# A two-layer streaming encoder on one core: first norm's sums by token, weights loaded between token blocks, two gap columns dropped

## The chip, the cores and the metric

One core of a Trainium2 chip runs the whole program. The metric is device time in microseconds (us) of one launch. The engines are TensorE (PE, matmuls; its weight loads are listed as PEld), VectorE (DVE), ScalarE (ACT), GpSimd (POOL) and SyncE (SP, which here only starts transfers). Transfers are started on three queues: SP's, ACT's and POOL's.

## The reference

1024 prompt tokens and 32 sample tokens of width 1024 go through two layers. Layer 0 mixes tokens by chunked attention with 16 heads and a learned relative-position bias, layer 1 by a gated MLP with position mixing (gMLP); a ConvFFN follows each mixer. All is float32.

```
def rms_norm(x, g):
    y = x * rsqrt(mean(x * x, axis=-1) + EPS)
    return y * g

# layer i (DEPTH = 2); prompt and sample tokens go the same way
h = rms_norm(x, ln_mix[i])
x = x + (band_attn(h) if i % 2 == 0 else gmlp(h))
x = x + conv_ffn(rms_norm(x, ln_ffn[i]))
...
y = rms_norm(x, ln_final)

def conv_ffn(h, hist, w_up, conv_w, conv_b, w_down):
    a = h @ w_up                         # 1024 -> 5632
    full = concat([hist, a])             # 2 rows of history (zeros for the prompt)
    c = conv_b + sum(full[:, j:j + T] * conv_w[j] for j in range(3))
    gate, val = split(c)
    return (silu(gate) * val) @ w_down
```

In attention a chunk of 64 queries sees its own and the 8 chunks before it: softmax(q k / 8 + bias) v, then `@ w_o`. The bias is a table of 257 distances per head.

## The kernel before, in words

**Layout.** Activations are kept transposed, features on the 128 partitions and tokens along the free axis: `x[P, 8, TW]`, with `TW` = 1058 columns: 1024 prompt tokens, 2 gap columns (`GAP`), 32 sample tokens. The gap holds zeros in `x`; in the ConvFFN's buffers it is the place of the sample's two history rows, so that one shifted access does the convolution of both. Columns are worked on in three chunks, `CH`, of 352, 352 and 354.

**Matmuls.** A product in float32 precision is three passes: the operand's high part (`gx_hi`, `w_hi`) and its rest (`gx_lo`, `w_lo`), as hi*hi + hi*lo + lo*hi (`product`, lines 156 to 158). A weight is split by ACT (`w_hi`, a copy with rounding) and DVE (`w_lo`, the difference). `linear` does the 8 feature tiles of a chunk, 24 matmuls. The norm's factor per token (`rstd`) is multiplied in as the product leaves PSUM, so PE need not wait for it; only `gx_hi` and `gx_lo` (x times the gain, lines 215 and 221) must be there.

**The start.** Nine token blocks (eight of 128 tokens, one of 32) arrive in token layout (`xin`), even ones on SP's queue and odd ones on ACT's. PE transposes each in two halves of four tiles (`turn_block`, line 381); ACT copies the first half to `x` (line 426) and DVE the second (line 444). A transpose of block b waits for the copies of block b - 2, which used the same PSUM banks. When a chunk's blocks are there, ACT makes, tile by tile, `gx_hi` and a square (`act_tile`, line 212), DVE `gx_lo`, and POOL adds the squares of the 8 tiles up in `total` (`Norm.pool`, lines 230 and 233). Two `squares` buffers stand between, so a square waits for the add of the one but one before it. A matmul with `ones` then sums over the partitions (`pe_sum`, line 238), and DVE, ACT and DVE again turn the sum into `rstd` over all 352 columns: mean, root, reciprocal.

**The steps.** The first head pair needs nine steps `first_pe(o)`, o from 0 to 8, a chunk of v, k or q each, in the order of `FIRST`: v and k of chunk 0, v and k of chunk 1, v and k of chunk 2, then q of all three. Steps use PSUM banks 6 and 7 in turn, so step o waits for the output of step o - 2 (`first_out`, lines 959 and 981). Steps 0 and 1 stand in `input_pe` behind block 5, the others behind block 8 in `attention_pe`; extra transposes of v, k and the parameters lie between the later ones.

**Other work at the start.** ACT's queue also loads the ConvFFN's taps and history (8 small loads). POOL makes constants, then stores the expanded bias table to DRAM (`bias_scratch`, 16 heads x 64 copies, line 367), waits for that, reads it back shifted into `bias` (line 371), and only then adds squares. SP issues the weights of v, k and q (`load_unit`, line 598) behind its token blocks; a slot of `raw0` is loaded again when its weight has been split.

**Behind it.** Eight head pairs of attention with the projections of the next pair laid between (a loop over pairs), ConvFFN 0 (22 feature pairs over two layers, 11 loop turns each: 12 groups of 24 matmuls up, 24 groups of 6 down), gMLP, ConvFFN 1, the last norm. The later norms sum by columns already (`pe_columns`, `dve_columns`, `pe_spread`): a matmul gives each token's sum on its own partition, the roots are taken there, and `ones` times a diagonal matrix of the factors (DVE, line 276) spreads them over the partitions again.

The order on each engine is written out by hand; semaphores tie them. Memory regions are shared over time: the attention's tiles lie where `xin` was, so what overwrites `xin` waits until it is read.

## Time and profile before

| | us |
|---|---|
| median of 3 runs | 2728.03 (2728.01 to 2732.96) |
| span of the profiled execution | 2726.1 |
| around the span, to the median (the profiled execution's own time is not listed) | 1.9 |
| PE busy | 2609.6 (96%) |
| DVE busy | 1610.8 (59%) |
| ACT busy | 902.6 (33%) |
| POOL busy | 256.6 (9%) |
| mean granted PE clock | 0.983 |

The span is from the first to the last instruction. Busy times of engines overlap. Matmuls are pipelined: an instruction's listed time is longer than the distance to the next, so the pace is read from starts. A granted clock of 1 is 2.4 GHz, 0.5 is 1.2 GHz.

### The profile page before, as it was taken

The numbers are of one execution on the slowest core, as the hardware profiler recorded it, in microseconds if no ns is written. First come the engines' busy times: TensorE is split into PE (matmuls) and PEld (weight loads), VectorE is DVE, ScalarE is ACT, GpSimd is POOL, SyncE is SP. The second block draws the span as 40 slices with busy tenths as digits, with TensorE's granted clock in tenths as the row PEclk, the third lists the DMA queues.
The fourth block names the chain that finished last, engine by engine and source line by source line (L and its number), as shares of the span: only waits on it lengthen the run. The fifth ranks groups of instructions, "written<-read, shape, count | busy, mean of one in ns | idle before, by whom it ended". The sixth has DMA issues, their size and how long they took to land.

```text
span 2726.1 us, 43489 instructions
## 1 busy us (share of the span) xinstructions
PE 2609.6 (96%) x15757; PEld 2524.9 (93%) x15757; DVE 1610.8 (59%) x3213; ACT 902.6 (33%) x1711; POOL 256.6 (9%) x583
## 2 busy tenths in 40 slices
PE   4999999999789999999999999999999999999998
PEld 4888888888669999999999999999899999999998
DVE  5565566656566666666666552332666666666666
ACT  4333433343353222222222353132522222222223
POOL 4000000000030000000000042122100000000003
PEclk8999999999889999999999999999999999999999
DMA  4111111110001111111111121111111111111111
GB/s 130 44 36 37 32 32 41 36 36 21 24 16 47 47 46 46 46 46 46 46 46 46 31 64 31 32 33 46 63 47 46 45 37 41 46 46 46 46 44 76
DMA packets 99451, 120.66 MB, mean 44 GB/s; under 512 B 3676, under 2 KB 87844, under 8 KB 99332
## 3 DMA queue, kind: packets, MB, share of 16 engines
q1 hardware_dynamic: 94972, 108.06, 12.3%
q0 software_dynamic: 3088, 8.67, 1.1%
q10 hardware_dynamic: 1272, 2.39, 0.3%
q8 instruction: 69, 1.13, 0.2%
q14 instruction: 50, 0.41, 0.0%
HBM read 108.70 MB, written 10.40 MB: 44 GB/s over the span
## 4 chain that ended last, share of the span: by engine, by line
PE 88%; DVE 4%; ACT 3%; POOL 2%; issue 2%; DMA 1%; DVEq 0%; ACTq 0%; POOLq 0%
PE psum L156 25%; PE psum L158 25%; PE psum L157 25%; PE psum L770 4%; PE psum L809 2%; PE psum L754 2%; POOL total L233 2%; PE psum L806 1%; PE psum L1588 1%; DVE x L1050 1%; DMA bias_scratch<-rel_rev 1%; DVE gx_lo L221 1%; PE psum L692 0%; ACT conv_t L1277 0%; ACT v L703 0%
## 5 line engine op out<-in xcount | busy, mean ns | idle before, releaser
L156 PE MATMUL psum<-gx_hi,w_hi 128*128 128x352 f32 (+1 forms) x3264 | 1075.6, 330 | 13.8 <-DVE stage L959 4.1
L158 PE MATMUL psum<-gx_hi,w_lo 128*128 128x352 f32 (+1 forms) x3264 | 1062.6, 326 | 0.0
L157 PE MATMUL psum<-gx_lo,w_hi 128*128 128x352 f32 (+1 forms) x3264 | 1062.5, 326 | 0.0
L156 PEld LDWEIGHTS psum<-gx_hi,w_hi 128*128 128x128 f32 x3264 | 618.9, 190 | 19.8 <-issue 8.0
L157 PEld LDWEIGHTS psum<-gx_lo,w_hi 128*128 128x128 f32 x3264 | 618.1, 189 | 2.3 <-issue 0.7
L158 PEld LDWEIGHTS psum<-gx_hi,w_lo 128*128 128x128 f32 x3264 | 619.4, 190 | 0.0
L1364 DVE TENSOR_TENSOR x<-x,psum 128x352 f32<-128x352 f32 (+1 forms) x528 | 259.7, 519 | 120.9 <-PE psum L158 120.9
L1277 ACT ACTIVATE conv_t<-a_gate,cur 128x352 f32<-128x352 f32 x132 | 90.1, 683 | 539.6 <-DVE a_gate L1334 539.3
L156 PE MATMUL psum<-h_hiA,w_hi 128*128 128x352 f32 (+1 forms) x528 | 171.8, 325 | 4.1 <-DVE x L1364 4.1
L156 PE MATMUL psum<-h_hiB,w_hi 128*128 128x352 f32 (+1 forms) x528 | 172.0, 326 | 0.0
L158 PE MATMUL psum<-h_hiA,w_lo 128*128 128x352 f32 (+1 forms) x528 | 171.1, 324 | 0.0
L157 PE MATMUL psum<-h_loA,w_hi 128*128 128x352 f32 (+1 forms) x528 | 170.8, 323 | 0.0
L157 PE MATMUL psum<-h_loB,w_hi 128*128 128x352 f32 (+1 forms) x528 | 170.6, 323 | 0.0
L158 PE MATMUL psum<-h_hiB,w_lo 128*128 128x352 f32 (+1 forms) x528 | 170.5, 323 | 0.0
L1169 DVE TENSOR_TENSOR w_lo<-raw,w_hi 128x1024 fp32r<-128x1024 f32 x132 | 160.9, 1219 | 12.3 <-ACT w_hi L1166 12.3
L1334 DVE TENSOR_TENSOR a_gate<-psum,rstd 128x352 f32<-128x352 f32 (+2 forms) x176 | 72.1, 431 | 146.2 <-PE psum L158 143.3
L1166 ACT ACTIVATE w_hi<-raw 128x1024 fp32r<-128x1024 f32 x132 | 136.0, 1045 | 2.0 <-PE psum L158 1.9
L1341 DVE SCALAR_TENSOR_TENSOR conv_t<-a_gate,cur,conv_t 128x352 f32<-128x352 f32 x132 | 77.4, 586 | 99.2 <-ACT conv_t L1277 99.0
L897 ACT ACTIVATE pT<-psum 128x512 f32<-128x512 f32 (+2 forms) x160 | 78.9, 505 | 155.4 <-PE psum L754 154.4
L770 PE MATMUL psum<-pT,v 128*128 128x256 f32 (+1 forms) x496 | 126.9, 386 | 0.0
L1277 ACT ACTIVATE conv_t<-a_val,cur 128x352 f32<-128x352 f32 x132 | 90.2, 683 | 105.0 <-DVE a_val L1334 105.0
L1282 ACT ACTIVATE s_gate<-conv_t 128x352 f32<-128x352 f32 x132 | 65.9, 499 | 165.9 <-DVE conv_t L1344 165.9
(180 smaller groups left out, 3447.2 us busy)
## 6 DMA issues: line engine op xcount, KB each, us to landing
raw<-in_f_w_up SPq DMA_DIRECT2D x44, 1024.0 KB, 5.1
raw<-in_f_w_down SPq DMA_DIRECT2D x22, 1024.0 KB, 4.9
raw<-in_a_w_qkv SPq DMA_DIRECT2D x24, 512.0 KB, 3.8
raw<-in_b_w_in SPq DMA_DIRECT2D x8, 1024.0 KB, 5.4
raw<-in_a_w_o SPq DMA_DIRECT2D x8, 512.0 KB, 3.5
raw<-in_b_w_out SPq DMA_DIRECT2D x4, 1024.0 KB, 5.0
out<-raw SPq DMA_DIRECT2D x6, 512.0 KB, 2.7
xin<-in_x_prompt SPq DMA_DIRECT2D x4, 512.0 KB, 5.4
```

The source lines that it names most:

```text
L156: pe.matmul(out, w[0], rhs[0], start=first, stop=False)
L157: pe.matmul(out, w[0], rhs[1], start=False, stop=False)
L158: return pe.matmul(out, w[1], rhs[0], start=False, stop=last)
L770: mm = pe.matmul(psum[:, bank, :width], v, pT[:rows, slot, 2 * P * i:2 * P * i + width], start=(kb == blocks[0]), stop=(kb == blocks[-1]))
L897: act.activation(dst, src, ACT.Copy).then_inc(t_free, 1)
L1166: act.activation(shape(f_hi[slot]), self.raw_of(u), ACT.Copy).then_inc(self.w_hi, 1)
L1169: dve.tensor_tensor(shape(f_lo[slot]), self.raw_of(u), shape(f_hi[slot]), ALU.subtract)\
L1277: act.activation(conv_t[:, o % 2, :n], a_buf[g][:, start + 2:start + 2 + n], ACT.Identity, scale=cur[:, 2, g, i:i + 1], bias=cur[:, 3, g, ...
L1282: act.activation(s_gate[:, start:start + n], conv_t[:, o % 2, :n], ACT.Silu).then_inc(self.silu, 1)
L1334: mm = dve.tensor_tensor(a_buf[g][:, a + 2:b + 2], psum[:, o % RING, a - start:b - start], rstd[:, a:b], ALU.mult)
L1341: dve.scalar_tensor_tensor(t, a_buf[g][:, start + 1:start + 1 + n], cur[:, 1, g, i:i + 1], t, ALU.mult, ALU.add).then_inc(self.conv1, 1)
L1364: mm = dve.tensor_tensor(chunk(x[:, d, :], c), chunk(x[:, d, :], c), psum[:, n % RING, :CH[c][1]], ALU.add)
```

## The change

The first norm is summed in token layout: as a block arrives, ACT squares it whole with an accumulator (`first_square`), which gives the token's sum on its partition in `rs_col`; its output goes to unused space in `bias`. For three groups of blocks (0 to 2, 3 to 5, 6 to 8) DVE takes the mean, ACT the root, DVE the reciprocal and the diagonal blocks, PE spreads them by a matmul with `ones`, ACT copies the result to `rstd`. POOL adds nothing here any more. ACT copies the first halves of blocks 0 to 2 alone; DVE copies both halves from block 3 on.

The v and k weights are loaded on SP's queue between token blocks; the taps and history go from ACT's queue to SP's. The bias store waits for token blocks 6 and 7, and SP reads it back, after the last square. Steps 0 and 1 stand behind block 4, and steps 2 to 4 between the later blocks.

`GAP` is no longer in `TW`: 1056 columns, three chunks of 352. The ConvFFN's buffers keep the gap (`AW`), so its convolution of the third chunk still has 354 columns, and the product of gate and value is written in two pieces there. Memory clears of the gap in `rstd`, `x`, `o_hi`, `o_lo` fall away.

```diff
-    TW = SEQ + GAP + DEC
-    SMP = SEQ + GAP
+    TW = SEQ + DEC
+    SMP = SEQ
+    AW = TW + 2 * GAP
     CH = [(0, 352), (352, 352), (704, TW - 704)]
+    CONV_N = [352, 352, TW + GAP - 704]
...
+    ACT_HALVES = 3
+    def turned_by_dve(b):
+        return b + 1 if b < ACT_HALVES else ACT_HALVES + 2 * (b - ACT_HALVES + 1)
...
+    FIRST_CUT = [(0, 3 * P), (3 * P, 6 * P), (6 * P, TW)]
+    def first_square(act, b):
+        n = BLOCKS[b][1]
+        act.wait_ge(x_in[b], 16)
+        at_least(act, first_sq, b)
+        junk = bias[:n, :, :].rearrange("p t v -> p (t v)")[:, :D]
+        act.activation(junk, xin[:n, b, :], ACT.Square, accum_out=rs_col[:n, b:b + 1]).then_inc(first_sq, 1)
+    def first_means(dve, g):
+        dve.wait_ge(first_sq, min(3 * g + 3, NB + 1))
+        for rows, cut in FIRST_COLS[g]:
+            dve.tensor_scalar(rs_col[rows, cut], rs_col[rows, cut], 1.0 / D, EPS, ALU.mult, ALU.add)\
+                .then_inc(first_mean, 1)
+    def first_inverse(dve, g):
...
+            dve.reciprocal(rs_col[rows, cut], rs_col[rows, cut]).then_inc(first_inv, 1)
+        dve.wait_ge(first_inv, FIRST_AT[g + 1])
+        for b in range(3 * g, min(3 * g + 3, NB + 1)):
+            start, n = BLOCKS[b]
+            op = dve.tensor_scalar(total[:n, start:start + n], ident[:n, :n], rs_col[:n, b:b + 1], None, ALU.mult)
+        op.then_inc(first_diag, 1)
+    def first_spreads(pe, g):
+        a, b = FIRST_CUT[g]
+        pe.wait_ge(first_diag, g + 1)
...
+        mm = pe.matmul(psum[:, 4, :last - a], ones[:, :], total[:, a:last], start=True, stop=True)
...
+    def first_rstd(act, g):
+        a, b = FIRST_CUT[g]
+        act.wait_ge(first_spread, g + 1)
+        act.activation(rstd[:, a:b], psum[:, 4, :b - a], ACT.Copy).then_inc(first_ready, 1)
 
     def input_sp(sp):
...
+        block(0)
+        block(2)
+        load_unit(sp, 0, 1, qkv_unit(2, 0))
+        block(4)
+        load_unit(sp, 1, 2, qkv_unit(1, 0))
+        block(6)
         sp.dma_start(xin[:DEC, NB, :], x_sample[0]).then_inc(x_in[NB], 16)
+        for i in range(DEPTH):                      # taps and history: 8 loads, from ACT's queue
...
+        load_unit(sp, 0, 3, qkv_unit(0, 0))
+        sp.wait_ge(rel_out, 16)
+        sp.wait_ge(first_sq, NB + 1)
+        for h in range(2):
...
+            sp.dma_start(bias[CK * h:CK * (h + 1), :, :], src).then_inc(bias_in, 16)
...
         pool.wait_ge(rel_done, 2)
+        pool.wait_ge(x_in[NB - 2], 16)
+        pool.wait_ge(x_in[NB - 1], 16)
         pool.dma_start(bias_scratch, rel_rev[:, None, :].to_broadcast([HEADS, CK, REV])).then_inc(rel_out, 16)
-        pool.wait_ge(rel_out, 16)
...
     def input_pe(pe):
         turn_params(pe, 0)
-        for b in range(NB + 1):
+        for b in range(5):
             turn_block(pe, b)
-            if b == LAST_BLOCK[1]:
-                first_pe(pe, 0)
-                norm_a.pe_sum(pe, 0)
-                first_pe(pe, 1)
+        first_pe(pe, 0)
+        first_pe(pe, 1)
+        first_spreads(pe, 0)
+        for b in (5, 6):
+            turn_block(pe, b)
+        first_pe(pe, 2)
+        first_spreads(pe, 1)
+        first_pe(pe, 3)
+        for b in (7, 8):
+            turn_block(pe, b)
+        first_pe(pe, 4)
+        first_spreads(pe, 2)
 
     def input_act(act):
...
+        for b in range(3):
+            block(b)                                # square, and the first half's copy for b < 3
+        split_act(act, 0)
+        halves(0)                                   # gx_hi of the chunk's 8 tiles
+        split_act(act, 1)
+        first_roots(act, 0)
+        block(3)
+        first_rstd(act, 0)
+        block(4)
+        block(5)
+        halves(1)
+        first_roots(act, 1)
+        block(6)
+        first_rstd(act, 1)
+        block(7)
+        block(8)
+        halves(2)
+        first_roots(act, 2)
+        first_rstd(act, 2)
 
     def input_dve(dve):
...
+        for b in range(3):
+            block(b)
+        split_dve(dve, 0)
+        halves(0)                                   # gx_lo
+        first_means(dve, 0)
+        split_dve(dve, 1)
+        block(3)
+        first_inverse(dve, 0)
+        block(4)
+        first_out(dve, 0)
+        block(5)
+        first_out(dve, 1)
+        first_means(dve, 1)
+        halves(1)
+        first_inverse(dve, 1)
+        block(6)
+        block(7)
+        first_out(dve, 2)
+        block(8)
+        first_means(dve, 2)
+        halves(2)
+        first_inverse(dve, 2)
...
     def attention_pe(pe):
-        for o in range(2, STEPS):
+        for o in range(5, STEPS):
             first_pe(pe, o)
-            if o in (3, 4):
-                norm_a.pe_sum(pe, o - 2)
-            if o in (4, 5):
-                turn_params(pe, o - 3)
-            if o == 5:
+            if o in (5, 6):
+                turn_params(pe, o - 4)
+            if o == 6:
...
-                        pr = prod[:, k_par(c, i), :n]
-                        dve.tensor_tensor(pr, t, s_gate[:, start:start + n], ALU.mult).then_inc(self.prod, 1)
+                        for a, b, at in self.pieces(c):   # two pieces in the third chunk
+                            cut = slice(at - GAP, at - GAP + b - a)
+                            mm = dve.tensor_tensor(prod[:, k_par(c, i), a - start:b - start],
+                                                   conv_t[:, o % 2, cut.start - start:cut.stop - start],
+                                                   s_gate[:, cut], ALU.mult)
+                        mm.then_inc(self.prod, 1)
```

## Rows read from the trace of the kernel before

**Rows 1.** Stretches: window, length, busy us (instructions) per engine, PE clock, DMA share, GB/s.
```profile
0.00:37.30 37.30, 10.70 (x49) 9.64 (x50) 11.56 (x16) 14.32 (x26) 12.68 (x22) 0.77 0.85 223
37.30:73.90 36.60, 29.00 (x154) 27.63 (x153) 23.98 (x28) 18.14 (x38) 18.02 (x18) 0.86 0.05 16
...
840.00:1550.00 710.00, 708.70 (x4385) 708.06 (x4385) 458.43 (x839) 205.82 (x311) 25.52 (x143) 1.00 0.14 46
```

**Rows 2.** Waits, 0 to 95 us: who <- released by: us, times, longest.
```profile
PE psum L381 <- ACT x L426: 17.1, 1, 17.1
...
POOL bias L371 <- DMA bias_scratch<-rel_rev: 15.7, 1, 15.7
...
ACT squares L212 <- POOL total L230: 8.1, 1, 8.1
```

**Rows 3.** Timeline (start, length): first matmuls of steps 0, 5 and of attention.
```profile
37.32 0.64 PE L156 MATMUL psum<-gx_hi,w_hi 128*128 128x352 f32 x1
...
73.97 0.41 PE L156 MATMUL psum<-gx_hi,w_hi 128*128 128x354 f32 x1
...
93.79 0.71 PE L806 MATMUL psum<-kT,qd 128*128 128x64 f32 x4 [1.02 <-DVE qd L981]
```

**Rows 4.** Transfers, 11 to 14 us: packets, MB per queue; issues: KB each, us to landing.
```profile
DMA packets 411, 1.13 MB, mean 378 GB/s; under 512 B 19, under 2 KB 175, under 8 KB 411
...
q10 hardware_dynamic: 165, 0.61, 56.6%
...
q1 hardware_dynamic: 161, 0.09, 10.6%
...
raw<-in_a_w_qkv SPq DMA_DIRECT2D x2, 512.0 KB, 23.8
...
bias<-bias_scratch POOLq DMA_DIRECT2D x2, 384.0 KB, 7.9
```

**Rows 5.** Lines, 0 to 95 us: count | busy us, mean ns | idle before.
```profile
L381 PE MATMUL psum<-ident,xin 128*128 128x128 f32 x64 | 12.8, 378 | 19.7 <-ACT x L426 17.1 <-DMA xin<-in_x_prompt 1.6 <-DVE x L444 1.0
...
L215 ACT ACTIVATE gx_hi<-x,gains 128x352 fp32r<-128x352 f32 x16 | 9.2, 576 | 3.3 <-DVE x L444 3.3
...
L444 DVE COPY x<-psum 128x512 f32<-128x512 f32 x8 | 5.3, 686 | 6.7 <-PE psum L381 6.7
...
L563 ACT ACTIVATE w_hi<-raw 128x1024 fp32r<-128x1024 f32 x4 | 4.1, 1043 | 0.0
...
L238 PE MATMUL psum<-total,ones 128*128 128x352 f32 x4 | 1.5, 458 | 0.0
```

**Rows 6.** Timeline of DVE: one gx_lo, and the nine diagonal blocks of a later norm.
```profile
16.63 0.59 DVE L221 SCALAR_TENSOR_TENSOR gx_lo<-x,gains,gx_hi 128x352 fp32r<-128x352 f32 x1 [0.28 <-ACT gx_hi L215]
...
817.40 1.80 DVE L276 TENSOR_SCALAR total<-ident,rs_col 128x128 f32<-128x128 f32 x9
```

**Rows 7.** Lines, 100 to 180 us: an accumulator's reading on ACT.
```profile
L922 ACT ACTIVATION_READ_ACCUMULATOR p_even<-psum,neg_max 128x1 f32 x8 | 1.5, 192 | 0.0
```

**Rows 8.** Timeline of PE, ConvFFN: starts of groups of 48, 24, 96 and 48 matmuls.
```profile
902.16 0.32 PE L156 MATMUL psum<-gx_hi,w_hi 128*128 128x352 f32 x1
...
909.90 0.32 PE L156 MATMUL psum<-gx_hi,w_hi 128*128 128x354 f32 x1
...
913.79 0.32 PE L156 MATMUL psum<-gx_hi,w_hi 128*128 128x352 f32 x1
...
925.43 0.33 PE L156 MATMUL psum<-h_hiA,w_hi 128*128 128x352 f32 x1
...
940.84 0.33 PE L156 MATMUL psum<-h_hiA,w_hi 128*128 128x354 f32 x1
...
948.68 0.32 PE L156 MATMUL psum<-gx_hi,w_hi 128*128 128x352 f32 x1
```

**Rows 9.** Timeline: gx_lo beside POOL's adds; POOL clearing qd.
```profile
59.22 3.54 DVE L221 SCALAR_TENSOR_TENSOR gx_lo<-x,gains,gx_hi 128x354 fp32r<-128x354 f32 x3
...
63.37 3.75 POOL L631 MEMSET qd<- 128x2176 f32 x2
```

More of the change, by code:

```diff
@@ L90, in build @@
     psum = ctx.enter_context(nc.psum_tensor("psum", [P, 8, BANK], F32))
-    squares = hold("squares", [P, 2, 354])
+    squares = hold("squares", [P, 2, 352])
     total = hold("total", [P, TW])
@@ L226, in pool @@
                 k = KT * c + d
-                pool.wait_ge(self.squared, self.tiles + k + 1)
+                pool.wait_ge(self.squared, self.sums + k + 1)
                 sq = squares[:, k % 2, :CH[c][1]]
@@ L231, in pool @@
                 else:
-                    pool.wait_ge(self.added, self.tiles + k)
+                    pool.wait_ge(self.added, self.sums + k)
                     pool.tensor_tensor(chunk(total, c), chunk(total, c), sq, ALU.add).then_inc(self.added, 1)
-        def pe_sum(self, pe, c):
-            pe.wait_ge(self.added, self.tiles + KT * (c + 1))
-            at_least(pe, self.mean, self.chunks + c)
-            pe.matmul(psum[:, self.bank, :CH[c][1]], ones[:, :], chunk(total, c), start=True, stop=True)\
-                .then_inc(self.summed, 1)
-        def dve_mean(self, dve, c):
-            dve.wait_ge(self.summed, self.chunks + c + 1)
-            dve.tensor_scalar(chunk(rstd, c), psum[:, self.bank, :CH[c][1]], 1.0 / D, EPS, ALU.mult, ALU.add)\
-                .then_inc(self.mean, 1)
-        def act_root(self, act, c):
-            act.wait_ge(self.mean, self.chunks + c + 1)
-            act.activation(chunk(rstd, c), chunk(rstd, c), ACT.Sqrt).then_inc(self.root, 1)
-        def dve_rstd(self, dve, c):
-            dve.wait_ge(self.root, self.chunks + c + 1)
-            dve.reciprocal(chunk(rstd, c), chunk(rstd, c)).then_inc(self.ready, 1)
         COLS = ((slice(0, P), slice(0, NB)), (slice(0, DEC), slice(NB, NB + 1)))
@@ new lines, in first_roots @@
+    def first_roots(act, g):
+        for k, (rows, cut) in enumerate(FIRST_COLS[g]):
+            act.wait_ge(first_mean, FIRST_AT[g] + k + 1)
+            act.activation(rs_col[rows, cut], rs_col[rows, cut], ACT.Sqrt).then_inc(first_root, 1)
+    def first_inverse(dve, g):
+        for k, (rows, cut) in enumerate(FIRST_COLS[g]):
+            dve.wait_ge(first_root, FIRST_AT[g] + k + 1)
+            dve.reciprocal(rs_col[rows, cut], rs_col[rows, cut]).then_inc(first_inv, 1)
[4 more added lines that the diff above has]
+        op.then_inc(first_diag, 1)
@@ new lines, in first_spreads @@
+    def first_spreads(pe, g):
+        a, b = FIRST_CUT[g]
+        pe.wait_ge(first_diag, g + 1)
+        at_least(pe, first_ready, g)
+        last = min(b, SEQ)
+        mm = pe.matmul(psum[:, 4, :last - a], ones[:, :], total[:, a:last], start=True, stop=True)
+        if b > SEQ:
+            mm = pe.matmul(psum[:, 4, SEQ - a:b - a], ones[:DEC, :], total[:DEC, SEQ:b], start=True, stop=True)
+        mm.then_inc(first_spread, 1)
+    def first_rstd(act, g):
+        a, b = FIRST_CUT[g]
+        act.wait_ge(first_spread, g + 1)
+        act.activation(rstd[:, a:b], psum[:, 4, :b - a], ACT.Copy).then_inc(first_ready, 1)
@@ L377, in turn_block @@
         for half in range(2):
-            at_least(pe, (x_act, x_dve)[half], b - 1)
+            if half == 0:
+                at_least(pe, x_act, min(b - 1, ACT_HALVES))
+            if b >= 2 and (half == 1 or b - 2 >= ACT_HALVES):
+                pe.wait_ge(x_dve, turned_by_dve(b - 2))
             for j in range(4):
@@ L438, in input_dve, with block, halves @@
-    def input_dve(dve):
+        first_pe(pe, 0)
[10 more added lines that the diff above has]
+        first_spreads(pe, 2)
+    def input_act(act):
+        def block(b):
+            first_square(act, b)
+            if b < ACT_HALVES:
+                act.wait_ge(x_turned, 2 * b + 1)
+                act.activation(*turned(b, 0), ACT.Copy).then_inc(x_act, 1)
+        def halves(c):
+            for d in range(KT):
+                norm_a.x_ready(act, c, d)
+                norm_a.act_hi(act, c, d)
+        copy_params(act, 0)
+        for b in range(3):
[17 more added lines that the diff above has]
+        first_rstd(act, 2)
@@ L439, in input_dve, with block, halves @@
+    def input_dve(dve):
+        def block(b):
+            for half in range(0 if b >= ACT_HALVES else 1, 2):
+                dve.wait_ge(x_turned, 2 * b + half + 1)
+                dve.tensor_copy(*turned(b, half)).then_inc(x_dve, 1)
+        def halves(c):
+            for d in range(KT):
+                norm_a.dve_tile(dve, c, d)
         dve.wait_ge(rel_in, 16)
@@ L984, in attention_dve @@
     def attention_dve(dve, norm):
-        norm_a.dve_row(dve, 1)
-        for o in range(2, STEPS):
-            if o == 4:
-                norm_a.dve_row(dve, 2)
+        for o in range(3, STEPS):
             if o == 6:
@@ L1616, in v_set @@
                 if first and o < 2:
-                    act.wait_ge(Norm.added, norm.tiles + NCH * KT)
+                    act.wait_ge(Norm.added, norm.sums + NCH * KT)
                 else:
@@ L1846, in y_sums @@
     def y_sums(pe, group):
-        pe.wait_ge(Norm.added, norm_e.tiles + KT * (NCH - 1 + group))
+        pe.wait_ge(Norm.added, norm_e.sums + KT * (NCH - 1 + group))
         for b in Y_GROUPS[group][0]:
@@ L1998, in _ @@
         input_pool(pool)
-        for c in range(NCH):
-            norm_a.pool(pool, c)
         attention_pool(pool)
```

155 lines of the change are left out of this document (57 added, 98 removed).

## The prediction

> **What bounds the kernel now.** I read the page first: TensorE (PE) is busy in 2609.6 of 2726.1 us, so the end can only move where PE stands idle or where its matmuls get shorter. The view by stretches says where it is idle [rows 1]: in 840 to 1550 us, the first ConvFFN, PE works 708.7 of 710.0 us and every other engine has slack (DVE 458.4); in the first 37.3 us it works 10.7, and in the next 36.6 us 29.0, at a granted clock of 0.86. So the change has two places: the start, up to the first attention matmul at 93.79 us [rows 3], and the width of the third chunk everywhere behind it.
>
> The view of waits over the start names the chain [rows 2]. PE's longest idle time, 17.1 us, ends when ScalarE (ACT) copies a transposed block. ACT was late because a square of the first norm waited 8.1 us for GpSimd (POOL) to add the one before, and POOL began to add only after 15.7 us of waiting for the bias table's store into DRAM, which stands ahead of the adds in its program. Then ACT still had squares and weight splits to do before PE's first projection step began at 37.32 us. The fifth further on, called step 5 (the steps count from 0), began at 73.97, and attention 19.8 us after that [rows 3].
>
> **The change part by part.** I rebuild the time of step 5 in the new order, because from there on PE's work is the old one.
>
> Loads. By the packet counts of 11 to 14 us each queue gets one packet in turn: 165 of ACT's and 161 of SP's, though 0.61 MB against 0.09, as a weight's packets are an eighth of a token block's [rows 4]. SP's queue now holds blocks 0 and 2, the v weight, block 4, the k weight, block 6. The v weight's 1024 small packets therefore outlast the 512 large ones of blocks 1, 3, 5, 7 on ACT's queue. So it lands when 3.67 MB are through: at 378 GB/s [rows 4] 9.7 us, from a start of the loads near 2.5 us, 12.2; I take 14.0, as ACT's queue starts later, behind the gains, and small packets end the transfer. Bounds: 8.5 if the queues shared by bytes, and 27.2, where it lands now (issue at 3.4 plus 23.8, [rows 4]) with the bias store beside it; the store now waits for blocks 6 and 7. The estimate is nearest to the first, since what slowed that row is gone. The k weight comes after another 1.05 MB, about 17.5, before ACT wants it.
>
> Step 0. Before 14.0 ACT has done three squares of whole token blocks and three copies, until 13.1; that it issues eight loads less ahead of them gains nothing, since it then waits for the weight. A square of 1024 columns is not in the trace; a split of that width takes 1.04 [rows 5] and reading an accumulator 0.19 [rows 7], so 1.25, not below 1.04 and not above 1.6 (a half again). PE has turned five blocks by 17.3 (12.8 us for eight blocks, [rows 5]). From 14.0: split of v 1.04, eight gx_hi of 0.576 [rows 5] to 19.7, split of k to 20.7. DVE follows with w_lo of v and eight gx_lo of 0.59 [rows 6], is through at 21.1, and makes w_lo of k (no longer than the gap of 1.2 to 22.4). Step 0 ends at 21.7 in their shadow. The square's adds on POOL, 24 of them, are gone, and with them the wait of 8.1.
>
> Steps 1 to 4. Step 1 from 22.4: 24 matmuls are 7.74 / 2 = 3.87 us [rows 8], with its drain 4.0, to 26.4. The spread of the first 384 columns takes 0.85 (the old sums of 352 columns took 0.75, 1.5 us for two, [rows 5]), the copy to rstd on ACT no more than a gx_hi, 27.9. Here is the new wait: ACT stands 3.4 us at that copy, and squares 4 and 5 (2.5 us) and eight gx_hi (4.6) queue behind it, to 35.0; the last gx_lo is done at 35.7, the three diagonal blocks cost DVE 0.6 (a third of 1.80, [rows 6]) and a reciprocal 0.16, 36.4. PE, which turned blocks 5 and 6 meanwhile and did step 2 at DVE's pace, spreads until 37.3 and does step 3 until 41.4. Then it turns blocks 7 and 8, 1.1 us to the second half; DVE copies both halves (0.69 each, [rows 5]) to 43.3, puts out step 2 (0.5, no more than a gx_lo) and copies the small block 8, 44.4; one gx_hi and eight gx_lo of the third chunk end at 49.7, the reciprocals and diagonals at 50.6, the spread at 51.5, where step 5 starts. I add 0.5 for PE's clock: PE will stand idle 2.1 us at 29.5 and 2.7 us at 43, and the stretch with such gaps now has 0.86 [rows 1]. So 52.0 instead of 73.97.
>
> To attention. From step 5 the old order took 19.8 us; a transpose of parameters (0.4) moves behind step 5 and a few copies stand differently, so 20.4: attention at 72.4 instead of 93.79. Saved: 21.4.
>
> What this costs elsewhere is nothing, under these covers. The bias band is read back by SP after the last square (40.4) and after the store, which starts at 20 and is waited for 15.7 us now [rows 2], so is through by 36; the two reads land about 7.9 us after issue [rows 4], near 49, and are wanted at 73. Behind those waits on SP stands one weight of the next head pair, wanted at 60. The parameters' loads, now on SP behind the tokens, are wanted at 56. Clearing qd on POOL (3.75 us, [rows 9]) lies at 44 to 48 beside DVE's gx_lo of the third chunk. Beside POOL's two-input adds gx_lo takes 1.18 [rows 9] instead of 0.59; the long clears of the trace lie beside one-input work only. A clear reads nothing, so I take 0, and keep 3.75 / 1.18 x 0.59 = 1.9 as the other end. The Trainium skill, GPSIMD Engine Reference, section Specifications, says that GpSimd shares its SBUF interfaces with VectorE and contends with instructions of two SBUF inputs, and exempts no kind of GpSimd work; gx_lo is such an instruction, so by that rule the 1.9 would be paid.
>
> Two columns less. A third-chunk group of 24 matmuls takes 913.79 - 909.90 = 3.89 us, one of 352 columns 3.87: 23 ns less in finer digits. In the down projection 48 matmuls of the third chunk take 7.84, of the others (940.84 - 925.43) / 2 = 7.71 [rows 8], of which I count only the same 23 ns a group, as the rest may belong to the loop's turn. Groups: ConvFFN 22 x (4 + 2) = 132, attention 8 x 4 = 32, gMLP 24: 188 x 23 ns = 4.3 us. Bounds: 0 (not the columns) and 22 x (130 - 46) ns more, 6.2. The Trainium skill, TensorE: Matmul & The Clock Gate, section Wait — 56ns, not 53.3ns?, gives N / 2.4 GHz + 2.5 ns from start to start: 149 ns for 352 columns, where the trace has 161 [rows 8], so its level does not hold here; its slope would make the saving 3.8.
>
> The extra half product per value tile on DVE (44 times) is hidden by the 251 us that DVE is free in 710 [rows 1]; uncovered, at a whole 0.59 each, it would be 26 us.
>
> The sum: -21.4 - 4.3 = -25.7. The profiled span of 2726.1 has some 1.9 us around it to the median of the runs, 2728.0; 2728.0 - 25.7 = 2702.3.
>
> **The rivals.** (a) The weights come late: each us of the v weight beyond 14.0 moves step 5 by one, as the chain starts there. For it: small packets lose by turns [rows 4]; against it: nothing is left beside them. At 18 to 24: 2706 to 2712. (b) PE's clock stays at the lower of its two levels until 26 us, through steps 0 and 1: step 1 then takes 7.0 instead of 3.9, and 0 is late too, 5.4 together: 2707.7. For it: [rows 1] has 0.77 for the first stretch; against it: PE now works from 7 us almost without a gap. (c) DVE pays beside the clears: 2704.2. (d) Slower: the bias band becomes the wait. DVE's first attention step needs both reads; if SP's smaller pieces and the store behind the tokens bring them past 73 + 25.7 = 99 us, the kernel loses one us per us: at 105, 2734. Against it: 58 us between issue and that point, where two reads take 7.9 now. (e) The start isn't shortened because another wait takes the gap, say the spread's copy in ACT's order holding blocks 7 and 8 back: only the columns stay, 2723.7 or no change.
>
> **How the numbers follow.** The forecast has 0.72, with an own range of 2698 to 2706; (a) 0.11, (b) 0.08, (c) 0.04, (d) 0.03, (e) 0.02. The range 2697 to 2711 reaches from both gains at their best (6.2 for the columns, the v weight by 13, where ACT is free, no clock loss: 2698.9, and some 2 us of what the parts leave open) into most of (a) and all of (b) and (c). 0.2% is 5.5 us, about what a measurement here can tell from no change. Faster by more than that: 0.95; within: 0.02; slower: 0.03.
>
> **What would show it.** Step 5's first matmul near 52 and attention near 72; POOL without adds before 80 us; the v weight's split starting at 14; ACT waiting some 3 us once, for the first spread; a third-chunk group at the length of the others. Wrong: the split of v after 18, step 1 at 7 us, gx_lo of 1.18 between 45 and 50, or DVE waiting for the bias.

## The result, and the profile after

The changed kernel takes 2695.94 us (median of 4 runs, 2693.13 to 2698.9) against 2729.01 for the kernel before beside it (2728.01 to 2732.96): a ratio of 0.9874, 95% interval 0.986 to 0.9888. That is 33 us less; the profiled spans, 2726.1 and 2691.4, differ by 34.7. The forecast was 25.7 less, and the time lies 1.1 us below the low end of the range. The direction was right, and the start saved about what was forecast, in part by luck; one term of the sum, the columns, was given a third of what it measured.

Stretches of the kernel after, to be held against [rows 1] (window, length, busy us and instructions of PE, PEld, DVE, ACT, POOL, PE clock, DMA share, GB/s):

```profile
0.00:37.30 37.30, 25.70 (x147) 23.48 (x148) 20.27 (x42) 24.25 (x45) 2.45 (x10) 1.00 0.83 202
37.30:73.90 36.60, 32.14 (x193) 30.75 (x192) 17.13 (x43) 12.94 (x28) 8.14 (x11) 0.91 0.35 88
840.00:1550.00 710.00, 705.71 (x4380) 705.12 (x4379) 458.55 (x857) 216.00 (x337) 40.25 (x155) 1.00 0.13 43
...
40.00:50.00 10.00, 7.45 (x34) 7.37 (x34) 7.12 (x21) 4.13 (x10) 3.77 (x2) 0.66 0.64 131
```

PE works 25.7 of the first 37.3 us instead of 10.7. The last row is the stretch in which its clock was at the lower of its two levels (0.66 on the mean): it fell at 42.3 us, while PE stood 2.55 us for the third chunk (40.7 to 43.2), and rose at 49.2.

PE's timeline after, against [rows 3] (start, length): first matmuls of steps 0 and 5 and of attention.

```profile
16.80 0.40 PE L157 MATMUL psum<-gx_hi,w_hi 128*128 128x352 f32 x1 [0.40 <-DVE gx_lo L216]
...
50.70 0.43 PE L157 MATMUL psum<-gx_hi,w_hi 128*128 128x352 f32 x1
...
70.77 0.32 PE L881 MATMUL psum<-kT,qd 128*128 128x64 f32 x1 [1.09 <-DVE qd L1055]
```

Attention starts 23.0 us earlier (93.79 - 70.77). The other 11.7 come behind it. PE's starts in the first ConvFFN, against [rows 8], matmul for matmul:

```profile
872.22 0.32 PE L157 MATMUL psum<-gx_hi,w_hi 128*128 128x352 f32 x1
...
879.90 0.32 PE L157 MATMUL psum<-gx_hi,w_hi 128*128 128x352 f32 x1
...
883.74 0.32 PE L157 MATMUL psum<-gx_hi,w_hi 128*128 128x352 f32 x1
...
895.26 0.32 PE L157 MATMUL psum<-h_hiA,w_hi 128*128 128x352 f32 x1
...
910.86 0.32 PE L157 MATMUL psum<-h_hiA,w_hi 128*128 128x352 f32 x1
...
918.63 0.32 PE L157 MATMUL psum<-gx_hi,w_hi 128*128 128x352 f32 x1
```

Read the distances: the third chunk's group took 3.89 and takes 3.84. But the 48 matmuls of the first two chunks, whose width is the same in both kernels, took 7.74 and take 7.68, and the 96 of the down projection with unchanged width went the other way, 15.41 to 15.60. So the pace changed of matmuls that the change leaves as they are. A whole turn of this loop took 69.79 us and takes 69.45; there are 22 turns, 7.6 us.

Over the whole trace PE's matmul time at full clock (busy time less half of what fell into stretches at the lower level) is 12.8 us less: some 7 of it in the two ConvFFNs, 3 in the gMLP between them, 2 in attention and the rest at the end. With the 23.0 of the start that is 35.8; idle time behind the start is 2.1 longer and the clock there costs 0.9 less, which leaves 34.6. These two can't be put to the change: in the last head pair alone, where PE idles some 24 us in every kernel of this study, the lower clock cost 13.6 us before, 9.1 after, and between 8 and 15 in the others. The start varies with the clock too: in the seven kernels below that keep the changed kernel's order and move only addresses or columns, attention began between 67.9 and 72.3 us.

### The profile page after: what moved, and what is told of

It reads as the page before. It is cut to its first block, busy times and chain, and to the rows that moved or that the text cites. A ratio compares the mean times of both kernels' runs of the same rounds, so it can differ in the third digit from the quotient of the medians.

```text
span 2691.4 us, 43514 instructions
## 1 busy us (share of the span) xinstructions
PE 2592.8 (96%) x15759; PEld 2509.1 (93%) x15759; DVE 1604.1 (60%) x3274; ACT 898.7 (33%) x1703; POOL 240.0 (9%) x553
## 4 chain that ended last, share of the span: by engine, by line
PE 88%; DVE 4%; ACT 3%; POOL 2%; issue 2%; DMA 0%; ACTq 0%; DVEq 0%; POOLq 0%
PE psum L157 25%; PE psum L159 25%; PE psum L158 25%; PE psum L845 4%; PE psum L884 2%; POOL total L228 2%; PE psum L829 2%; PE psum L881 1%; PE psum L1666 1%; DVE x L1121 1%; DVE gx_lo L216 1%; PE psum L770 0%; ACT conv_t L1350 0%; ACT v L781 0%; DVE gx_lo L1825 0%
## 5 line engine op out<-in xcount | busy, mean ns | idle before, releaser
L157 PE MATMUL psum<-gx_hi,w_hi 128*128 128x352 f32 x3264 | 1073.3, 329 | 17.1 <-DVE gx_lo L216 7.0
L158 PE MATMUL psum<-gx_lo,w_hi 128*128 128x352 f32 x3264 | 1058.4, 324 | 0.0
L159 PE MATMUL psum<-gx_hi,w_lo 128*128 128x352 f32 x3264 | 1057.8, 324 | 0.0
L1442 DVE TENSOR_TENSOR x<-x,psum 128x352 f32<-128x352 f32 x528 | 258.9, 516 | 122.4 <-PE psum L159 122.4
L157 PE MATMUL psum<-h_hiA,w_hi 128*128 128x352 f32 x528 | 172.3, 326 | 4.3 <-DVE x L1442 4.3
L157 PE MATMUL psum<-h_hiB,w_hi 128*128 128x352 f32 x528 | 172.5, 327 | 0.0
L159 PE MATMUL psum<-h_hiB,w_lo 128*128 128x352 f32 x528 | 171.9, 326 | 0.0
L159 PE MATMUL psum<-h_hiA,w_lo 128*128 128x352 f32 x528 | 171.4, 325 | 0.0
L158 PE MATMUL psum<-h_loA,w_hi 128*128 128x352 f32 x528 | 170.6, 323 | 0.0
L158 PE MATMUL psum<-h_loB,w_hi 128*128 128x352 f32 x528 | 170.4, 323 | 0.0
```

What stands on the lines that cost most here:

```text
L157: pe.matmul(out, w[0], rhs[0], start=first, stop=False)
L158: pe.matmul(out, w[0], rhs[1], start=False, stop=False)
L159: return pe.matmul(out, w[1], rhs[0], start=False, stop=last)
L1442: mm = dve.tensor_tensor(chunk(x[:, d, :], c), chunk(x[:, d, :], c), psum[:, n % RING, :CH[c][1]], ALU.add)
```

## The experiments

**Where the pace comes from.** The tiles lie one behind the other in a partition, so a narrower row moves all that follows: by the tiles' sizes, rows of `gx_hi` and `gx_lo` stand 4224 bytes apart in the changed kernel (33 x 128) and 4232 before, and its weights (`raw0`, `w_hi`, `w_lo`) begin 32 bytes beyond a multiple of 64, where they began on one before. "Turn" is the distance of one matmul in two turns of the ConvFFN loop, "up" (1024 to 5632 features) and "down" (back to 1024) the mean distance of matmuls in ns, worked out from starts over a turn's 288 and 144; they come out alike in every turn, to 0.05 us. "Weights" says where the tiles begin: x64 at a multiple of 64 bytes, +32 beyond one by 32. "Single" marks one run; a time also holds what the clock cost in that execution, so the reading goes by the turn. (Some expectations quote 160.3 up and 161.6 down for the kernel after; those means had taken in matmuls of the neighbouring group. The table has it right: 160.0 and 162.3.)

| kernel | columns | rows apart | weights | turn us | up | down | time us |
|---|---|---|---|---|---|---|---|
| before | 1058 | 4232 | x64 | 69.79 | 161.6 | 161.5 | 2729.0 |
| before_pitch1064 | 1058 | 4256 | x64 | 69.74 | 161.4 | 161.5 | 2726.0 |
| before_pitch1072 | 1058 | 4288 | x64 | 69.80 | 161.6 | 161.5 | 2728.1 |
| before_cols | 1056 | 4224 | +32 | 69.45 | 160.0 | 162.3 | 2718.8 |
| after | 1056 | 4224 | +32 | 69.45 | 160.0 | 162.3 | 2695.9 |
| after_n354 | 1056, up 354 | 4224 | +32 | 69.71 | 160.9 | 162.2 | 2705.4 single |
| after_pitch1058 | 1056 | 4232 | +32 | 70.02 | 161.9 | 162.4 | 2715.2 |
| after_pitch1064 | 1056 | 4256 | +32 | 69.89 | 161.5 | 162.4 | 2711.3 |
| after_w01 | 1056 | 4224 | up x64, down +32 | 69.18 | 159.0 | 162.4 | 2679.9 single |
| after_w64 | 1056 | 4224 | x64 | 68.73 | 159.2 | 159.0 | 2682.7 |
| w64_pitch1058 | 1056 | 4232 | x64 | 69.32 | 161.2 | 159.0 | 2694.4 single |
| w64_pitch1072 | 1056 | 4288 | x64 | 69.27 | 160.9 | 159.3 | 2691.9 single |

before_cols: the column hunks of the diff alone, on the kernel before.

> The kernel before with the two gap columns dropped and nothing else: the start, its sums, loads and order are the old ones. From here on the pace is read from one turn of the ConvFFN loop, the distance of the same matmul in two turns, 69.79 us before and 69.45 after. Theory (the third term of the sum, the columns, was mis-sized and is worth 12.7 us at full clock, not 4.3): the turn falls to 69.45 and the time to 2716, 12 to 14 us less, while attention still starts near 93.8. Rival (the columns are worth the 4.3 that the prediction gave them, and the rest of the gain comes from the start or from chance in the clock): the turn falls to 69.65, the time to 2724 to 2725.

Turn 69.45; 2718.8 us, ratio 0.9966 (0.9952 to 0.998). PE's work at full clock fell by 13.0, as after; attention began 2.0 us later (95.78 against 93.79). The time fell by 11.2 against the kernel before beside it (2730.0), a little under the 12 to 14 expected. The first theory holds: the columns' hunk is worth some 13 of PE's work, and the start the rest. The first matmuls of two turns:

```profile
942.96 0.32 PE L158 MATMUL psum<-gx_hi,w_hi 128*128 128x352 f32 x1
...
1012.41 0.32 PE L158 MATMUL psum<-gx_hi,w_hi 128*128 128x352 f32 x1
```

after_pitch1058, after_pitch1064, before_pitch1064, before_pitch1072: only the distance of rows.

```
-    gx_hi = hold("gx_hi", [P, KT, TW], F32R)
+    gx_hi = hold("gx_hi", [P, KT, 1058], F32R)[:, :, :TW]     # gx_lo alike; 1064, 1072 in the others
```

> The changed kernel with its 1056 columns, but the rows of gx_hi and gx_lo stand 1058 columns apart as before (4232 bytes instead of 4224; 4224 is a multiple of 64, 4232 is not). Same instructions, same columns, only the addresses of the moving operand differ. Theory (the row distance sets the pace of all groups, the narrow ones too: 161.25 ns from matmul to matmul before against 159.98 after at the same 352 columns): the groups go back to 161.2 or so, the turn of the ConvFFN to 69.7, the time rises by 6 to 9 us, to 2702 to 2705. Rival (fewer columns and lighter traffic of the other engines make the pace): turn 69.45, time 2696, as after.

> The changed kernel with rows of gx_hi and gx_lo 1064 columns apart (4256 bytes, a multiple of 32 and not of 64). Theory of the row distance, first form (every row must begin at a multiple of 64 bytes): half the rows are off, so the turn lies between 69.5 and 69.7 and the time 3 to 6 us over the changed kernel's. Second form (multiples of 32 do): turn 69.45, time 2696. Rival (the row distance is nothing): 69.45 and 2696 as well, but then the run with 1058 shows it too.

> The kernel before with its 1058 columns and its old start, and only the rows of gx_hi and gx_lo 1064 columns apart instead of 1058 (4256 bytes instead of 4232). Theory of the row distance, if multiples of 32 bytes do: the groups of 352 columns go from 161.25 to 160.0 ns a matmul, the turn falls from 69.79 to 69.5, the time by 6 to 9 us to 2720 to 2723, with not one column less. If multiples of 64 are wanted: about half of that. Rival (columns alone): turn 69.79, time 2728 to 2729.

> The kernel before with all its 1058 columns and its old start; only the rows of gx_hi and gx_lo stand 1072 columns apart (4288 bytes, a multiple of 64; to make room rel_rev lies where kout is written later). Theory (rows must begin at multiples of 64 bytes; the columns themselves are worth next to nothing): the groups of 352 columns go from 161.4 to 160.0 ns a matmul, those of 354 to 160.9, the turn of the ConvFFN falls from 69.79 to 69.46 us, and the time to 2717 to 2719, like that of the kernel with the columns dropped, with not one column less. Rival (it takes the 1056 columns, or another address that moved with them): turn 69.74 to 69.79, time 2726 to 2730.

In the changed kernel the distance matters, and more than expected: with rows 4232 apart it is at 2715.2 (0.9951 of before, 0.9934 to 0.9969), with 4256 at 2711.3, where 2702 to 2705 and 2699 to 2702 were expected; and its turn of 70.02 with 4232 is worse than before's though it has fewer columns. Some other address had to be at fault too. In the kernel before the distance gives little (2726.0 with 4256) or nothing (4288): that expectation of mine failed, and the form "a multiple of 64 is enough" with it. Here are the first matmuls of two turns of after_pitch1058:

```profile
949.49 0.32 PE L157 MATMUL psum<-gx_hi,w_hi 128*128 128x352 f32 x1
...
1019.51 0.32 PE L157 MATMUL psum<-gx_hi,w_hi 128*128 128x352 f32 x1
```

after_w64 and after_w01: the weights.

```
+    hold("gap0", [P, 8])                          # 32 bytes, in both
     raw0 = hold("raw0", [P, 2048])
```

after_w64 has 32 bytes more ahead of `h_hiA`, after_w01 96 behind the second `w_lo` instead.

> The changed kernel with 32 unused bytes ahead of raw0, so that the weights' tiles raw0, raw1, w_hi and w_lo begin at multiples of 64 bytes as before (in the changed kernel they begin 32 beyond one); 32 more ahead of h_hiA keep the h tiles where they were, at multiples of 64. Theory (weights off the 64 bytes cost as rows of gx do: the run with 1058 columns between rows had a longer turn than before, 70.02 against 69.79, though its columns are fewer, and the weights' addresses are what was left): the second feature pair's group and the down projection, which still vary (161.25 and 161.64 ns), come to 160.0 to 161, the turn falls from 69.45 to 69.1 to 69.3, the time by 3 to 8 us to 2688 to 2693. Rival (only rows of the moving operand count, weights are loaded whole beside the matmuls): turn 69.45, time 2696.

> The changed kernel with 32 unused bytes ahead of raw0 and 96 behind the second w_lo, so that only raw0, w_hi and w_lo 0 and 1 move onto multiples of 64 bytes; these are the weights of the 12 groups up. Everything else (squares, total, the ConvFFN's and the h tiles, and the weights of the down projection) keeps its place modulo 64. Theory (the address of the weights that a matmul loads sets its pace): the groups up go from 160.3 to 159.0 ns a matmul as in the run with all weights moved, the down projection stays at 161.6; turn 69.06 to 69.1. Rival (the other engines' tiles, which moved too in that run, disturbed PE's reads less): groups up stay at 160.3, turn 69.45.

after_w64 runs in 2682.7 us, 0.983 of before (0.9813 to 0.9846), 13 us under the changed kernel, for 32 bytes that nobody reads; that is more than the theory gave (turn 68.73 against 69.1 to 69.3, time 2688 to 2693). Its timeline over one turn, up from 916.34 and down from 962.18:

```profile
916.34 0.32 PE L158 MATMUL psum<-gx_hi,w_hi 128*128 128x352 f32 x1
...
962.18 0.33 PE L158 MATMUL psum<-h_hiA,w_hi 128*128 128x352 f32 x1
...
985.08 0.32 PE L158 MATMUL psum<-gx_hi,w_hi 128*128 128x352 f32 x1
```

after_w01 splits it within one run: the groups up, whose weights moved, go from 160.0 to 159.0; the down projection, whose weights and tiles kept their place, stays at 162.4. Its timeline (groups up from 936.94 and 983.22, down from 959.83):

```profile
936.94 0.32 PE L159 MATMUL psum<-gx_hi,w_hi 128*128 128x352 f32 x1
...
959.83 0.33 PE L159 MATMUL psum<-h_hiA,w_hi 128*128 128x352 f32 x1
...
983.22 0.32 PE L159 MATMUL psum<-gx_hi,w_hi 128*128 128x352 f32 x1
...
1006.12 0.32 PE L159 MATMUL psum<-gx_hi,w_hi 128*128 128x352 f32 x1
```

983.22 to 1006.12 is 22.90 us for 144 matmuls, 159.0 each; 959.83 to 983.22 is 23.39 for as many, 162.4. So the address of the weights acts on the pace by itself. The single time of after_w01 is no measure of it: its turns are 0.27 us shorter than after's, 6 us over 22, and the other 10 of its 16 us go mostly with the clock: the lower level cost it nothing at the start, where it cost the kernel after 3.0, and 22.3 behind it instead of 29.0.

w64_pitch1058 and w64_pitch1072: both at once.

> The kernel with all weights at multiples of 64 bytes, and only the rows of gx_hi and gx_lo 1058 columns (4232 bytes) apart instead of 1056. Theory (the place of the moving rows sets the pace as the weights' place does, each on its own): the groups up go from 159.1 back to 161 or so, as before (161.6 and 160.9 for its groups of 352), the down projection stays at 159.1; turn 69.3 to 69.4. Rival (once the weights stand well the rows don't matter): 159.1 both, turn 68.73.

> The kernel with all weights at multiples of 64 bytes, and rows of gx_hi and gx_lo 1072 columns (4288 bytes, a multiple of 64 and not of 128) apart. The kernel before with this distance gained nothing (161.0 and 160.4 ns in its groups of 352, 163.3 in those of 354). Theory 64 (multiples of 64 do; what held that run up was its 354 columns and other tiles): groups up stay at 159.1, turn 68.73. Theory 128 (rows must begin at multiples of 128 or at least all alike): groups up at 160.4 to 161, turn 69.1 to 69.3.

With good weights the rows still count: 4232 gives 161.2 up, 4288 gives 160.9, and 4224 gives 159.2, while the down projection, whose rows were left alone, stays at 159.0 to 159.3. One turn of w64_pitch1058:

```profile
920.60 0.32 PE L158 MATMUL psum<-gx_hi,w_hi 128*128 128x352 f32 x1
...
967.03 0.32 PE L158 MATMUL psum<-h_hiA,w_hi 128*128 128x352 f32 x1
...
989.92 0.32 PE L158 MATMUL psum<-gx_hi,w_hi 128*128 128x352 f32 x1
```

Theory 128 holds so far as that goes: of the three distances run with such weights (4256 was not) only the multiple of 128 gave the best pace. The down projection's rows all begin 64 beyond a multiple of 128 in after_w64 and do as well, so rows that are all alike may be what counts; that was not tried.

after_n354: the two columns by themselves, at the same addresses.

```
+            rhs = (wide(flat_hi, k), wide(flat_lo, k)) if more else ...   # 354 columns, up, third chunk
```

> The changed kernel, every tile at its place modulo 128, but the ConvFFN's groups up of the third chunk stream 354 columns again (the two more are the next row's first, and nobody reads what comes of them). So it measures the two columns by themselves, 88 groups of 24 matmuls. As in the prediction (23 ns a group, 0.96 ns a matmul): the group goes from 3841 to 3864 ns, the turn of the ConvFFN from 69.45 to 69.54 us. If the columns bring more than their share of time (one more line of the tile to read, as 163.3 against 160.7 ns in the groups of 354 and 352 of the kernel before with rows 1072 apart): 3900 to 3920 ns a group, turn 69.7. In either case the groups of 352 columns stay at 160.0.

```profile
950.50 0.32 PE L159 MATMUL psum<-gx_hi,w_hi 128*128 128x352 f32 x1
...
958.18 0.32 PE L159 MATMUL psum<-gx_hi,w_hi 128*128 128x354 f32 x1
...
962.08 0.32 PE L159 MATMUL psum<-gx_hi,w_hi 128*128 128x352 f32 x1
```

The group of 354 takes 3.90 us against 3.84 in the kernel after, in finer digits 3902 against 3841: 61 ns, not 23. The groups of 352 beside it stay at 160.0 to 160.2. That is the second theory's size; its reason, one more line to read, is not shown.

**What made the start.** after_bias_early and after_weights_late undo one part each, before_adds_first does one on the kernel before.

```
 after_bias_early:   -        pool.wait_ge(x_in[NB - 2], 16); pool.wait_ge(x_in[NB - 1], 16)
 after_weights_late: blocks 0, 2, 4, 6, sample, then load_unit of v and k
 before_adds_first:  pool.wait_ge(rel_out, 16) and the two reads behind norm_a.pool(pool, c)
```

> The changed kernel with one edit undone: the bias table's store into DRAM doesn't wait for token blocks 6 and 7 and is issued near 7 us again, beside the token blocks and weights. Theory (its bytes are in the way: before, block 7 landed at 23.4 and the v weight at 25.7, and now by 18.2 and 13.8): the v weight lands 3 to 6 us later, step 0 begins at 20 to 23 instead of 16.8, attention at 74 to 77 instead of 70.8, time 2699 to 2702. Rival (the store hurt only because POOL's adds waited behind it, and the adds are gone): step 0 at 16.8 to 17.5, time 2696.

2701.6 us, step 5 at 57.04, attention at 77.07: with the bytes of the store in the way the start is 6.3 us longer, part of it by the clock (three stretches of 3.4 us at the lower level against one of 6.8). But the bytes did not act where I had put it. The v weight landed at 12.9, as after (12.35); block 4 landed at 19.3 instead of 14.3, so step 0 began at 20.4, and ACT then waited for the k weight:

```profile
ACT w_hi L647 <- DMA raw<-in_a_w_qkv: 6.5, 1, 6.5
```

> The changed kernel with one edit undone: the v and k weights are issued on SP's queue behind all its token blocks and the sample, as before, not between them. Theory (the chain starts with the v weight, as the prediction's rival (a) said: one us later is one us later): the weight lands near 17.5 instead of before 13.9, step 0 begins at 20 to 21, step 5 at 53 to 55 instead of 50.7, time 2698 to 2701. Rival (ACT has squares left to do meanwhile, and PE's wait for the third chunk takes it up): step 0 late by 3 to 4, but step 5 at 51 and the time 2696 to 2697.

2699.5 us, step 0 at 19.33, step 5 at 53.91. The v weight landed at 16.35; ACT was free for it at 13.85, so 2.5 of its 4 us counted, and step 0 moved by as much. Step 5 moved by 3.2 and the time by 3.6; the further 0.7 lies within what the clock does to a start (at the lower level for three stretches of 3.4 us here, for one of 6.8 in the kernel after). So rival (a) of the prediction is real, about one for one, counted from the moment ACT is free.

> The kernel before with one edit at the start: POOL issues the bias table's store as before, but waits for it and reads it back behind the first norm's adds, not ahead of them. Nothing else moves. Theory (the long idle time of PE at the start was that wait, reached through the squares): the 8.1 us of ACT for POOL's first add go, step 0 begins at 29 to 30 instead of 37.3 and attention near 86, time 2720 to 2723; the rest of the 23 us is then the weights' and the sums' part. Rival (the weights, which landed at 25.7 and 29.4 behind the store, are the next wait, and POOL's adds beside DVE and the bias band that comes later take the rest back): step 0 at 33 to 36, time 2726 to 2730.

2723.7 us, ratio 0.9976 (0.9967 to 0.9986): step 0 begins at 31.14 and attention at 88.63, 5.2 us earlier. That lies between the theory (29 to 30, near 86) and the rival (33 to 36): the long wait on POOL, by itself, was about a quarter of the start's gain. What is late next is PE's wait for a transposed block, and behind it the v weight, which landed at 25.5:

```profile
PE psum L383 <- ACT x L428: 12.6, 1, 12.6
```

**Two better versions.** after_order_w64 has the weights' 32 bytes and another order at the start; `final` adds one wait on POOL.

```
 input_pe:   step 1; turn 5; spread 0; turn 6, 7, 8; step 2; spread 1; steps 3, 4; spread 2
 input_act:  squares 3 to 5, roots 1, squares 6, 7, rstd 0, gx_hi of chunk 1, copies 6, 7, square 8, ...
+        pool.wait_ge(first_diag, 3)               # final: ahead of the clears of qd
```

> The best version I can form from the runs: all weights at multiples of 64 bytes, and a new order at the start. PE turns block 5 ahead of the first spread and blocks 6, 7, 8 ahead of step 2 (block 8 into a bank of its own), then does steps 2, 3 and 4 in a row; ACT squares blocks 3 to 7 while it would wait for the first spread and copies the first halves of blocks 6 and 7; DVE makes the second group's diagonals before the third group's copies. Theory (in the changed kernel PE stands 2.3 us for gx_lo of the second chunk and 2.6 for the third, and pays 3.0 more as its clock falls to half from 42.3 to 49.2): step 2 at 29 to 30, step 5 at 42 to 44 instead of 50.0, attention at 62 to 64 instead of 70.1, time 6 to 8 us under the 2682.7 of the run with the weights moved alone, so 2674 to 2677. Rival (ACT, with two more copies and a square ahead of the third chunk, or DVE is late instead): step 5 at 47 to 50, time 2679 to 2683.

2672.7 us, 0.9792 of before (0.9778 to 0.9805), a little better than expected: step 5 at 43.95, attention at 63.95. The clock stayed at its upper level through this start; against after_w01, where it did too and attention began at 67.86, the new order is worth 3.9. One thing went against plan: DVE's last three diagonal blocks took 3.5 us instead of 0.6 to 0.7. DVE's and POOL's timelines (start, length):

```profile
25.28 0.68 DVE L351 TENSOR_SCALAR total<-ident,rs_col 128x128 f32<-128x128 f32 x3
...
34.44 3.77 POOL L719 MEMSET qd<- 128x2176 f32 x2 [15.91 <-DVE x L523]
...
35.00 3.50 DVE L351 TENSOR_SCALAR total<-ident,rs_col 128x128 f32<-128x128 f32 x3
...
39.13 0.40 PE L158 MATMUL psum<-gx_hi,w_hi 128*128 128x352 f32 x1 [1.56 <-DVE gx_lo L217]
```

> The version with the weights at multiples of 64 bytes and the new order of the start, and POOL's clear of qd held until DVE has made the third group's diagonals. In that version the three diagonal blocks took DVE 3.5 us instead of 0.6 while POOL cleared qd from 34.4 to 38.2, and PE then stood 1.56 us for gx_lo of the third chunk; eight gx_lo beside the same clear in the changed kernel took 0.58 each as ever. Theory (a one-input DVE instruction of that kind and the clear exclude each other, a two-input one and the clear don't): the diagonals take 0.6 to 0.7, gx_lo stay at 0.57 beside the clear, step 4 begins at 37.4 to 37.6 instead of 39.13, step 5 at 42.3 to 42.5 instead of 43.95, time 1.5 us less. Rival (the clear is paid by gx_lo instead): gx_lo at 1.2, step 5 at 44, no gain.

```profile
35.17 0.62 DVE L351 TENSOR_SCALAR total<-ident,rs_col 128x128 f32<-128x128 f32 x3
...
35.72 4.04 DVE L217 SCALAR_TENSOR_TENSOR gx_lo<-x,gains,gx_hi 128x352 fp32r<-128x352 f32 x8
...
35.90 3.77 POOL L720 MEMSET qd<- 128x2176 f32 x2 [17.04 <-DVE total L351]
...
42.26 0.43 PE L158 MATMUL psum<-gx_hi,w_hi 128*128 128x352 f32 x1
```

The diagonals take 0.62 again, the gx_lo beside the clear 4.04 for eight as without it, and step 5 begins at 42.26. The time is 2670.6 us, 0.9781 of before (0.9768 to 0.9795); the step of 1.7 shows in the trace, in the times (2672.7 to 2670.6) it is within their spread. This version is some 25 us faster than the changed kernel.

## Why the prediction missed

**The term that failed** is "Two columns less". It took the difference of a group of 354 and a group of 352 in the old trace, 23 ns, as the price of two columns, times 188 groups: 4.3, at most 6.2. PE's work fell by 12.8. after_n354 gives the price at equal addresses, for the ConvFFN's groups up: 61 ns. (188 x 61 ns would be 11.5, but the down projection, attention and gMLP were not tried.) The old trace hid it because its groups of 352 were themselves slow (7.74 us for 48, 161.25 ns each, where after has 160.0 and after_w64 159.2): their rows stood 4232 bytes apart. w64_pitch1058 shows that this is enough: with weights at multiples of 64, as before, and that distance alone put back, the groups up are at 161.2 again. The reference of the subtraction was spoilt, and the bounds, 0 to 6.2, came from the same rows. The prediction also treated the groups of unchanged width as unchanged; of the 347 ns of a turn they gained 70 (249 up, less 178 lost down, where the weights now stood 32 beyond), and the third chunk's six groups the other 277 instead of 138. Outside the ConvFFN the prediction had 0.6 for the gMLP and 0.7 for attention, where the traces have some 3 and 2; which of their groups gained was not looked into.

The Trainium skill, TensorE: Matmul & The Clock Gate, section Wait — 56ns, not 53.3ns?, has a pace of N / 2.4 GHz + 2.5 ns; its slope would make two columns 20 ns a group, where after_n354 has 61, and its level for 352 columns is 149 ns, where the best of the kernels here has 159.0. The measurements decide against both.

**The start** was forecast to save 21.4 and saved 23.0. Two errors of the sum offset each other, overlap and clock, so the agreement is in part luck. By its steps:

- The v weight's split began at 13.85, forecast 14.0, but not for the forecast reason. The weight landed at 12.35 and waited for ACT, whose squares and copies took until then (forecast 13.1); the prediction had the weight end that wait. Its load sum, 12.2, also came out by luck: it let the weight outlast all four blocks of ACT's queue, and blocks 5 and 7 landed after it, at 13.49 and 15.06. Packet counts as of one packet of each queue in turn stand from 9 to 12.35 us (278 of SP's, 283 of ACT's), but not from 6 to 9, where SP's queue (q1) moved far more packets than ACT's (q10; packets, MB, share):

```profile
q1 hardware_dynamic: 755, 0.65, 69.7%
q10 hardware_dynamic: 115, 0.46, 41.3%
```

- Step 1 began at 21.47 (22.4) and the spread's copy at 26.24 (27.3 to 27.9), with ACT waiting 3.8 for it (3.4): the new wait was there, at its place. It was not the only one: ACT waited 1.4 and 4.8 for the other two spreads, and the 4.8, behind the third chunk, cost PE nothing before step 5. Step 3 at 34.89 (37.3). The sum ran long mainly because an eight of gx_hi was counted as 8 x 0.576: 0.576 is one instruction's length, but they overlap, and eight take 3.95.

```profile
14.98 3.95 ACT L210 ACTIVATE gx_hi<-x,gains 128x352 fp32r<-128x352 f32 x8
...
16.07 4.05 DVE L216 SCALAR_TENSOR_TENSOR gx_lo<-x,gains,gx_hi 128x352 fp32r<-128x352 f32 x8
```

- PE's clock took part of that back: 0.5 was allowed, and PE at the lower level between 42.3 and 49.2 cost 3.0. So step 5 began at 50.70 (52.0). The tail to attention was 20.07 (20.4). These 3.0 do not come with the order of the start alone: in after_w01, with the same order, the clock stayed up and attention began at 67.86, 2.9 earlier. Its stretch against the last row of the result above:

```profile
40.00:50.00 10.00, 7.42 (x44) 6.55 (x43) 7.80 (x22) 5.49 (x12) 3.77 (x2) 1.00 0.56 123
```

- POOL's clear beside gx_lo: taken as 0, bound 1.9. Here gx_lo ran at 0.58 beside it, as before. The rule that the prediction weighed, from the Trainium skill, GPSIMD Engine Reference, section Specifications, would have had it paid; the trace doesn't agree for a clear. The Trainium skill, SBUF — State Buffer, section Who interferes with whom, is finer: an instruction of VectorE with two SBUF inputs contends with GpSimd work that reads SBUF, not with work that only writes it, and a `tensor_scalar` can contend in a 2-port mode, where whoever comes second is blocked whole. The runs agree with both so far as they go, 0.58 for a gx_lo and 3.5 for the diagonals; in which mode the diagonals ran, no run shows.
- The bias band was not waited for, DVE's extra half product stayed hidden (458.55 us busy in 710), POOL made no add before 80: right.

Of the rivals, (a) is real as a price (after_weights_late) and did not occur; (b), the clock, came at another place for 3.0; (c), (d) and (e) did not come.

## What to carry to other kernels

A price taken as the difference of two groups is only as good as the cheaper group: look whether that one stands at its own best pace, by its starts in several places, before subtracting. When a tile's width changes, work out where every later tile of the partition lands and whether rows and weights keep their alignment; here 32 unused bytes ahead of the weights were worth 13 us of 2696, more than the columns were forecast to be. And an eight of short instructions is timed from first start to last end, not as eight lengths.

## What the hardware showed that I had not expected

- The pace of a float32 matmul of 352 columns goes from 159.0 to 163.3 ns by the addresses of its weights and moving rows, at full clock (most groups of the down projection's first chunk have 163.3 in the kernel after and some 159 in after_w64). Which rule is behind it stays open: weights at multiples of 64 were better than 32 beyond (159.0 against 160.0 up, 159.0 against 162.3 down); rows 4224 apart were better than 4232, 4256 and 4288.
- DVE's diagonal blocks (one input tile and a scalar per partition) were held up by POOL's clear: in after_order_w64 they began at 35.00, the clear ended at 38.21 and they at 38.50, 3.5 us instead of 0.62; the clear itself took 3.77 with and without them. In the changed kernel the two did not meet, as the clear ended at 45.7 and the diagonals began at 46.7.
- The bytes of the bias store cost the start about as much as the wait for it: issuing it early again cost the changed kernel 5.7 us (2701.6 against 2695.9), and taking the wait alone off the kernel before gained 6.6 (2730.3 to 2723.7; 5.2 at attention). Each start is read from one trace, and starts of one order differ by up to 4.5 us, mostly with the clock, so the two are alike no closer than that.
